# The first two modulation kinds loaded and summed in two column halves, in a two-layer backbone step

## The reference, cut to what matters

```python
def modulation(cond, w, b):
    m = jax.nn.silu(cond) @ w + b
    return [t[:, None, :] for t in jnp.split(m, MOD_CHUNKS, axis=-1)]

def adaln_layer(x, cond, mod_w, mod_b, norm_g, w1, w2, mixer):
    sh1, sc1, gt1, sh2, sc2, gt2 = modulation(cond, mod_w, mod_b)
    h = rms_norm(x, norm_g[0]) * (1 + sc1) + sh1
    mix, aux = mixer(h)
    ...
# layer 0's mixer starts with
    z = h @ w_in          # 1024 -> 2304 columns
```

## Time and profile before

| | us |
|---|---|
| median of 3 runs | 2729.3 (2728.51 to 2731.03) |
| the profiled execution | 2729.33 |
| its span (first to last instruction) | 2727.5 |
| TensorE busy in the span | 2620.1 |
| VectorE busy | 1752.6 |
| ScalarE busy | 1367.5 |
| last block of mod_w taken up by TensorE | 40.08 |
| first panel product | 45.03 |
| first late modulation product, after unit 2 | 70.35 |

### The profile page before, as it was taken

The page is one execution under the profiler, slowest core; times in us unless marked ns, Lnnn a source line. Parts: engine busy times, 40 slices in busy tenths (PEclk is TensorE's granted clock), DMA queues, the critical chain, the costliest instruction groups (busy, mean ns, idle before and its releaser), DMA issues.

```text
span 2727.5 us, 38454 instructions
## 1 busy us (share of the span) xinstructions
PE 2620.1 (96%) x14907; PEld 2299.7 (84%) x14907; DVE 1752.6 (64%) x2805; ACT 1367.5 (50%) x2364; POOL 195.2 (7%) x180
## 2 busy tenths in 40 slices
PE   5999999999999999999999998889999999999998
PEld 3778888889998999788898887777899989998886
DVE  4246666664557777779721467985645577877787
ACT  5134445554444555554622676665544445554444
POOL 0000000000000000000000006982000000000000
PEclk8999999999999999999999999999999999999999
DMA  7653232634343554756523451015344344556565
GB/s 279 201 157 109 86 102 62 198 114 124 123 123 110 190 166 151 245 153 221 160 70 88 148 164 60 16 55 193 124 123 123 119 130 146 182 169 218 176 209 190
DMA packets 268608, 393.86 MB, mean 144 GB/s; under 512 B 25830, under 2 KB 207532, under 8 KB 267404
## 3 DMA queue, kind: packets, MB, share of 16 engines
q1 hardware_dynamic: 262192, 373.68, 43.0%
q10 hardware_dynamic: 4220, 9.86, 1.0%
q0 software_dynamic: 2016, 7.86, 0.7%
HBM read 331.98 MB, written 59.38 MB: 143 GB/s over the span
## 4 chain that ended last, share of the span: by engine, by line
PE 81%; DVE 6%; POOL 4%; ACT 4%; DMA 2%; issue 2%; SPq 1%; ACTq 0%; DVEq 0%; POOLq 0%
PE ps L2651 21%; PE ps L2764 15%; PE ps L2820 15%; PE ps L2729 9%; PE ps L2465 8%; PE ps L2855 4%; PE ps L2426 3%; POOL gap L952 2%; PE ps L2519 2%; POOL gap L953 2%; PE ps L2546 1%; PE ps L2482 1%; SPq L658 1%; ACT prT L1130 1%; DVE t_g L1873 1%
## 5 line engine op out<-in xcount | busy, mean ns | idle before, releaser
L1678 DVE TENSOR_TENSOR p_lo<-p_raw,p_hi 128x1024 fp32r<-128x1024 f32 (+1 forms) x299 | 367.4, 1231 | 340.8 <-ACT p_hi L1041 334.0
L1041 ACT ACTIVATE p_hi<-p_raw 128x1024 fp32r<-128x1024 f32 x267 | 280.1, 1053 | 224.4 <-DMA p_raw<-mlp_w 118.2
L2820 PE MATMUL ps<-p_hi,hq_hi 128*128 128x512 f32 x672 | 209.0, 392 | 11.8 <-DVE c_sum L2031 4.6
L2820 PE MATMUL ps<-p_lo,hq_hi 128*128 128x512 f32 x672 | 207.3, 390 | 0.0
L2820 PE MATMUL ps<-p_hi,hq_lo 128*128 128x512 f32 x672 | 207.3, 390 | 0.0
L2764 PE MATMUL ps<-t_hi,w_hi 128*128 128x384 f32 x512 | 172.7, 337 | 11.0 <-DVE c_sum L2031 11.0
L2764 PE MATMUL ps<-t_lo,w_hi 128*128 128x384 f32 x512 | 172.5, 337 | 0.0
L2764 PE MATMUL ps<-t_hi,w_lo 128*128 128x384 f32 x512 | 172.5, 337 | 0.0
L2729 PE MATMUL ps<-hm_hi,p_lo 128*128 128x384 f32 x512 | 172.1, 336 | 0.0
L2729 PE MATMUL ps<-hm_hi,p_hi 128*128 128x384 f32 x512 | 171.9, 336 | 0.0
L2729 PE MATMUL ps<-hm_lo,p_hi 128*128 128x384 f32 x512 | 171.6, 335 | 0.0
(11 more groups left out here) (329 smaller groups left out, 6437.2 us busy)
## 6 DMA issues: line engine op xcount, KB each, us to landing
p_raw<-mlp_w SPq DMA_DIRECT2D x208, 512.0 KB, 3.5
hq_raw<-hid_scratch SPq DMA_DIRECT2D x112, 384.0 KB, 4.1
mod_p<-mod_w SPq DMA_DIRECT2D x80, 512.0 KB, 4.2
w_pair<-mlp_w SPq DMA_DIRECT2D x32, 1024.0 KB, 5.9
p_raw<-gla_w_in SPq DMA_DIRECT2D x56, 512.0 KB, 3.6
hid_scratch<-c_out SPq DMA_DIRECT2D x128, 192.0 KB, 1.9
hid_scratch<-s_out SPq DMA_DIRECT2D x96, 192.0 KB, 1.9
p_raw<-gla_w_out SPq DMA_DIRECT2D x24, 512.0 KB, 3.4
```

What stands on the lines that cost most here:

```text
L1041: nc.scalar.activation(p_hi[s][:, :, 0:width], p_raw[s][:, :, 0:width], ACT.Copy).then_inc(pan_hi, 1)
L1678: V.tensor_tensor(p_lo[s][:, :, 0:width], p_raw[s][:, :, 0:width], p_hi[s][:, :, 0:width].bitcast(F32), ALU.subtract).then_inc(pan_lo, 1)
L2820: mm = M.matmul(acc(t)[:, 512 * to:512 * (to + 1)], x[layer][n % 4][:, half, t * P:(t + 1) * P], flat(w[s])[:, 512 * half:512 * (half + 1) ...
```

## The change

The eight blocks are loaded in two column halves. Half 0 of a block holds columns 0 to 511 of both kinds, which serve h chunks 0 to 3; half 1 holds columns 512 to 1023, for chunks 4 to 7. A half is [128, 2, 512], 512 KB, in two runs of 2 KB per row. SP now issues x groups 0 and 1, all first halves, the first panel, all second halves, x group 2, the second panel. The second halves reuse the semaphores of earlier transfers, and SP waits for the earlier transfer before it issues each.

The order of h chunks is now FRONT: groups 0 and 1 with chunks 0 to 3, groups 0 and 1 with chunks 4 to 7, then group 2. Sums, turn, add and weighing are done once per half. Unit 0 and unit 1 stop after four chunks and are finished later in their banks; the second halves' sums stand between the chunks of unit 1, two blocks after each. Squares and scaling of x group 2 stand behind the second sums. The semaphore values behind this move up by one or eight, and `mod_a` is cleared once at the start.

```diff
-    mod_w = [at(f"mod_w{i}", [P, 2 * D], F32, (RA, RC)[i // 4] + 8192 * (i % 4)) for i in range(DC)]
+    mod_w = [[at(f"mod_w{x}{i}", [P, 2, CONV], F32, (RA, RC)[i // 4] + 18432 * x + 4096 * (i % 4)) for i in range(DC)]
+             for x in range(2)]
...
+        FRONT = ([(g, c) for half in range(2) for g in range(2) for c in range(CC * half, CC * (half + 1))]
+                 + [(2, c) for c in range(DC)])
+        second_landed = [(first_in[0], 32), (first_in[1], 16), (cond_in, 48), (const_in, 16 * N_CONST)]
+        second_landed += [(mod_landed[b], 16) for b in range(DC - len(second_landed))]
...
+            def first_mod(half, b):
+
+                src = io["mod_w"][0][P * b:P * (b + 1), 0:2 * D].rearrange("p (a h n) -> p a h n", a=2, h=2)
+                if half:
+                    sp.wait_ge(*second_landed[b])
+                    sp.dma_start(mod_w[1][b][:], src[:, :, 1, :]).then_inc(second_landed[b][0], 16)
+                else:
+                    sp.dma_start(mod_w[0][b][:], src[:, :, 0, :]).then_inc(mod_landed[b], 16)
...
-            for b in range(3):
-                first_mod(b)
+            for b in range(DC):
+                first_mod(0, b)
+            in_panel(0)
+            for b in range(DC):
+                first_mod(1, b)
             first_x(2)
-            for b in range(3, 6):
-                first_mod(b)
-            in_panel(0)
-            for b in range(6, DC):
-                first_mod(b)
             in_panel(1)
...
+            def mod_sums(half):
+
+                act.wait_ge(modp_used, DC * (half + 1))
+                for j in (half, half + 2):
+                    last = nc.scalar.activation(mod_a[32 * j:32 * (j + 1), :], ps[32 * j:32 * (j + 1), ROWS_BANK, :], ACT.Copy)
+                last.then_inc(mod_rows, 1)
...
+            first_square(0)
+            first_square(1)
+            mod_sums(0)
             panel_split_hi(0)
...
+            for n in range(DC):
+                first_take(n)
+            mod_sums(1)
+            first_square(2, (0, 1))
+            act.wait_ge(mods_ready, 2)
+            for n in range(DC, 2 * DC):
+                first_take(n)
+                if n == DC + 1:
+                    first_square(2, (2,))
...
-            first_scale(2)
             split_lo(0)
...
+            first_add(0)
+            for n in range(DC):
+                first_split(n)
+            first_add(1)
+            first_scale(2, (0, 1))
+            for n in range(DC, 3 * DC):
+                first_split(n)
+                if n == DC + 1:
+                    first_scale(2, (2,))
+                if n == 2 * DC - 1:
                     split_lo(1)
...
+            def first_mod(half, b):
...
+                for i, j in enumerate((half, half + 2)):
+                    last = M.matmul(ps[32 * j:32 * j + MOD_ROWS, ROWS_BANK, :], csil[:, b, :], mod_w[half][b][:, i, :],
+                                    start=(b == 0), stop=(b == DC - 1))
+                last.then_inc(modp_used, 1)
...
+            def second_mods(c):
+
+                turn_ahead()
+                first_mod(1, 2 * c)
+                first_mod(1, 2 * c + 1)
...
+            turn_mods(0)
+            unit(0, lambda c: turn_ahead(), range(0, CC))
+            unit(1, second_mods, range(0, CC))
+            turn_mods(1)
+            unit(0, lambda c: turn_ahead(), range(CC, DC))
+            unit(1, lambda c: turn_ahead(), range(CC, DC))
+            unit(2, lambda c: turn_ahead())
```

More of the change, by code:

```diff
@@ L1041, in panel_split_hi, with first_square @@
                 nc.scalar.activation(p_hi[s][:, :, 0:width], p_raw[s][:, :, 0:width], ACT.Copy).then_inc(pan_hi, 1)
-            def first_square(g):
-                for t in range(GT):
+            def first_square(g, tiles=range(GT)):
+                for t in tiles:
                     i = GT * g + t
@@ L1679, in split_lo, with first_scale @@
                                 ALU.subtract).then_inc(pan_lo, 1)
-            def first_scale(g):
-                for t in range(GT):
+            def first_scale(g, tiles=range(GT)):
+                for t in tiles:
                     i = GT * g + t
@@ L1710, in _, with weigh, first_add, first_split @@
             own(last)
-            first_scale(2)
             split_lo(0)
[L1713 to L1728, removed]
+            def weigh(layer, kind, norm, plus, c0=0, c1=DC):
+                g = vec2[:, 32 * layer + 8 * norm + c0:32 * layer + 8 * norm + c1].unsqueeze(2).broadcast_to([P, c1 - c0, 2])
+                x = mods[:, layer, kind, c0:c1]
+                return V.scalar_tensor_tensor(out=x, in0=x, scalar=plus, in1=g, op0=ALU.add, op1=ALU.mult)
+            def first_add(half):
+                m = mods[:, 0, 0:2].rearrange("p a (j i) k -> p (a j) i k", i=4)[:, half::2]
+                x = ps[:, TURN_MODS, :].rearrange("p (i j r) -> p j i r", i=4, j=4)[:, half::2, :, 0:2]
+                dve.wait_ge(mod_turned, half + 1)
+                own(V.tensor_tensor(m, x, m, ALU.add))
+                weigh(0, 1, 0, 1.0, CC * half, CC * (half + 1)).then_inc(mods_ready, 1)
+            def first_split(n):
+                g, c = FRONT[n]
+                turn_split(h0[g], c, act_makes_hi(g, c))
+            first_add(0)
[8 more added lines that the diff above has]
+                if n == 2 * DC - 1:
                     split_lo(1)
@@ L2451, in used_before, with unit @@
                     late[0] = 0
-            def unit(u, between=None):
+            def unit(u, between=None, chunks=range(DC)):
                 p, n = divmod(u, GROUPS)
                 b, s = u % UNIT_BANKS, p % 3
-                if n == 0:
+                if n == 0 and chunks[0] == 0:
                     pe.wait_ge(pan_lo, T.next(pan_lo))
@@ L2460, in unit @@
                     pe.wait_ge(*reads(u - UNIT_BANKS))
-                for c in range(DC):
+                for c in chunks:
                     if p == 0:
-                        pe.wait_ge(h_ready, DC * n + c + 1)
+                        pe.wait_ge(h_ready, FRONT.index((n, c)) + 1)
                     for w, x in ((p_hi, 0), (p_hi, 1), (p_lo, 0)):
@@ L2549, in output @@
                 outputs[0] = p + 1
-            ahead = [(g, c) for g in range(GROUPS) for c in range(DC)]
+            ahead = list(FRONT)
             def turn_ahead():
@@ L2556, in turn_ahead, with turn_mods @@
                     first_turn(*ahead.pop(0))
+            def first_mod(half, b):
+                if half:
+                    done, value = second_landed[b]
+                    pe.wait_ge(done, value + 16)
+                else:
+                    pe.wait_ge(mod_landed[b], 16)
+                for i, j in enumerate((half, half + 2)):
+                    last = M.matmul(ps[32 * j:32 * j + MOD_ROWS, ROWS_BANK, :], csil[:, b, :], mod_w[half][b][:, i, :],
+                                    start=(b == 0), stop=(b == DC - 1))
+                last.then_inc(modp_used, 1)
+            def turn_mods(half):
+                pe.wait_ge(mod_rows, half + 1)
+                if half:
+                    pe.wait_ge(mods_ready, 1)
+                for i in range(4):
+                    last = turn(ps[:, TURN_MODS, i * P:(i + 1) * P], mod_a[:, i * P:(i + 1) * P])
+                last.then_inc(mod_turned, 1)
+            def second_mods(c):
+                turn_ahead()
+                first_mod(1, 2 * c)
+                first_mod(1, 2 * c + 1)
             pe.wait_ge(csil_ready, 1)
```

38 lines of the change are left out of this document (16 added, 22 removed).

## The result

| | before | after |
|---|---|---|
| median of 18 runs each, us | 2731.07 (2728.51 to 2732.66) | 2734.94 (2733.0 to 2739.57) |
| profiled execution, us | 2729.33 | 2733.0 |
| its span, us | 2727.5 | 2731.1 |
| first late modulation product, us from the start | 70.28 | 73.45 |

The ratio is 1.0020, 95% interval 1.0014 to 1.0026. The medians lie 3.9 us apart (0.14%), the means 4.7 (0.17%). The forecast was 2732.6, +3.3, in a range from 2727.5 to 2738.5: the sign, the place and nearly the size are right. Whether it counts as "within 0.2%" can't be told: the interval holds 0.2% in its middle.

A forecast was written before the change was run, and what follows sets the result against it. TensorE is busy 96%, so only the point from which it works without a gap counts. First product 12.1 us earlier, ninth chunk 1.5 later, 1.8 more behind it: +3.3, 2732.6 us, range 2727.5 to 2738.5.

The forecast's parts named there:

- first late modulation product: Point in TensorE's chain behind which the instruction sequence is unchanged; forecast at 73.7 us instead of 70.35, +3.3.
- within 0.2%: Whole-kernel time: 0.2%, or 5.5 us, taken as what a measurement can tell from no change; chance of same 0.66.
- Transfers: Load queue at the start: 1.40 us per half load, second halves landed at 38.2, SP's eight new waits priced at nothing.
- The hidden price of half loads: TensorE's column-group loads: a half load costs as much as a whole one, 1.76 us at 1.2 GHz, 0.95 at 2.4.
- First sums to first product: Two copies, panel rounding, VectorE's remainder, add and weighing in a row, from 27.0 to the first product at 32.9 us.
- The clock: TensorE's clock: up at about 19.7 us, low again after idling before the first product, high from the fourth chunk.
- Squares: ACT's squares of x group 2, brought out from under the loads: 2.7 us ahead of the ninth chunk, 1.4 behind it.
- B: Rival: clock stays at 1.2 GHz under two-group loads; +9.3 us, 2738.6, or about +19, 2748, with unit 1 low; chance 0.22.
- D: Rival: two column groups cost half a load on TensorE; -3.8 us, 2725.5; chance 0.12 including lighter forms.
- C: Rival: each half load pays a lone load's latency, 4.2 us; second sums 32 us later, 2764; chance 0.02.
- a shift of the point is added to 2729.3 directly: Reference: the shift of TensorE's gap-free point adds to the 2729.3 us median, the profiled execution having taken 2729.33.
- half of that stretch: Kernel before, behind the first product: TensorE said to run slowly for half the stretch, granted clock 0.51 from 44 to 51 us.

The follow-up runs named there:

- e3: Changed kernel with each half load summed in four column groups of 256 columns instead of two of 512; 2730.36 us, ratio 0.9999.
- e1: Changed kernel with squares and scaling of x group 2 moved ahead of the second sums; 2731.89 us, ratio 1.0009.
- e2: Changed kernel with three second loads' products moved into TensorE's hole before the first panel product, the other five after one chunk each; 2730.56 us, ratio 1.0007.
- e7: Changed kernel with four-group half loads, x group 2 queued and squared earlier, three second loads in TensorE's first hole; 2725.34 us, ratio 0.9981 to the kernel before.
- e8: The kernel with all three cures, plus two useless 128x512 products in TensorE's second hole; 2725.66 us, ratio 0.9983 to the kernel before.

## Why the prediction was right

| step | predicted | measured |
|---|---|---|
| half load's transfer | 1.40 | 1.35 (e3) |
| first load taken | 15.7 | 15.12 |
| half load on TensorE, low and full clock | 1.76, 0.95 | 1.78, 0.92 to 0.96 |
| first sums complete | 27.0 | 26.8 |
| first product | 32.9 | 32.80 |
| unit 0's four chunks done | 39.0 | 38.7 |
| unit 1's four chunks with loads | 11.0 | 11.4 |
| second sums complete | 50.0 | 50.05 |
| ninth chunk split | 54.9 | 55.1 |
| first late product | 73.7 | 73.45 |

- **Transfers.** The half loads ran through a full queue at 387 GB/s (15 to 20 us). No second load made TensorE wait; it was late for them, as forecast. SP's waits cost nothing visible (DMA share 1.05 or more in the rows from 15 to 50). x group 2 had landed by 41.2 (e1), a microsecond ahead of the estimate.
- **The hidden price of half loads.** It was the largest term, and the bounds in the prediction left a factor of two. 1.91 for two loads, and e3's 1.07, put it at the value taken.
- **First sums to first product.** The two copies (1.19), the panel's rounding (28.05) and VectorE's remainder (29.21, 1.23) stood one behind the other as summed.
- **The clock.** Low behind both holes, 33 to 37.3 and 56 to 61; full under the loads of unit 1 (0.99).
- **Squares.** They stand in the chain as forecast, two ahead of the ninth chunk and one behind. Moving all three away returned 2.6, not the 4.1 that the sum gave them. For the two ahead it was 1.73, not 2.7, because the turn, add and weighing that they covered then came out: ACT waited 1.16 us for them in e1. For the third it was 0.89, not 1.4; why, no run shows.
- **Compensating errors.** A pair of loads with its chunk lasted 2.89 us (45.23 to 48.12), not 2.75, because a chunk behind a load lasted 1.05 (0.72 + 0.33 in the chain) instead of 0.85. Unit 0 ended 0.3 sooner than forecast, having begun 0.1 sooner and its clock having risen earlier, so the second sums were met all the same. That is luck in part: five executions with the same instructions up to there copied the first sums at 26.2 to 27.2, by where the clock rose.
- **Rivals.** B, the low clock under two-group loads, fell: 0.99 from 37.3 to 50. D, loads at half price, fell by 1.78 and 0.92 per load; e3 shows that the same bytes can be had at half. C, a lone load's latency for each half, fell: the loads were taken 1.35 us apart, not 4.2. The rule behind C, in the Trainium skill, page "DMA: Bandwidth & Descriptors", section "Bandwidth", asks for batches of at least 1 MiB; here pieces of 512 KB at 387 GB/s took 12% more time per byte than at the 434 of the earlier trace rows, and none of it on TensorE's path, so a full queue does not bear the rule out.
- **What was too small.** The measured 2734.94 is 2.3 above the forecast. 1.8 of it is the reference: 2729.3 by three runs, 2731.07 by eighteen. The front, too, was read from one execution of before, with its late product at 70.28 (70.35 in the chain). The second profile had it at 68.84: the first product stood at 44.61 instead of 45.03, and the low clock behind it ended at 47.7 instead of 51. Against the mean of the two the shift is 3.7, not 3.2, and the medians gave 3.9 and 4.0. The weakest step is thus the reference: "a shift of the point is added to 2729.3 directly" took one execution's front, and all that lies behind it, for fixed.
- **A slip.** TensorE ran slowly not for "half of that stretch" behind the first product but for 6 us of 25 (45 to 51 of 45 to 70). No term of the sum rests on it.

## What to carry to other kernels

Cutting loads in two to start earlier paid here only as far as the pieces cost half on every engine that handles them: keep all column groups filled with narrower pieces (1.07 against 1.91 us for two), and copy, turn and add once per piece on full partitions. Then ask what lay beneath the wait that is removed, since it comes out on the path (here two squares and the panel's split), and put the work that is left over into the new holes. That can also keep TensorE's clock up (first product at 0.41 instead of 0.66 us in e2 and e7), though not in every execution (0.69 in e8). Each cure alone left the time within about 2 us of the kernel before; all of them turned +3.9 us into -5.3.

## What the runs showed of the hardware

- A chunk of three matmuls and a turn took 1.05 us where it stood between column-group loads, and 0.85 elsewhere (0.72 + 0.33 against 0.53 + 0.33 in the chain of the kernel after). By the starts, most of the 0.2 lies ahead of the load: from the turn to what follows it is 0.42 (39.02 to 39.44) where a load comes next and 0.25 (38.17 to 38.42) where a product does. It is the same where a load fills four groups: in e3 the period of two loads (1.00) and a chunk is 2.05 (40.39 less 38.34). What the change costs its time in, the traces don't show.
- From 15 to 20 us the granted clock is given as 1.00, but half loads last 1.78 us there (5.34 for three) and 0.92 from 20.7 on; the 1.2 GHz level, by their length. The trace's clock records begin only at 20.5 us, with a rise to full, and where there is no record the column says 1.00. For the first stretch of a program the durations have to be read, not that column.
- The same gap of TensorE is followed by a spell at the low clock in one execution and not in the next, with the same instructions. One such spell costs 1.7 to 1.8 us (0.91 over 20 us, 0.83 over 10). With the waits that differ too (1.15 and 2.40 near 1603), two profiles of the kernel after end 2.8 us apart. A single profile therefore tells differences of the whole span only to some 3 us, and where one stretch stands to a microsecond or so (68.84 and 70.28, 73.01 and 73.45), though what takes the time in a stretch stands in it to tenths.
